# Two-block transformer on one core: the second block's first adaptation summed by VectorE in the first feed-forward

## What is computed

```python
def adaln(cond, w, b):
    m = jax.nn.silu(cond) @ w + b
    return jnp.split(m, 3, axis=-1)
...
    shift, scale, gate = adaln(c[:, None, :], w_ada, b_ada)
    cshift, cscale, cgate = adaln(c_ctx, w_ada, b_ada)
    h = rms_norm_2(x, norm_g) * (1 + scale) + shift
```

```python
    h = rms_norm(x, ln2_gain)
    x = x + jnp.square(jax.nn.relu(h @ w_up)) @ w_down
```

## Time and profile before

| | |
|---|---|
| median of three runs | 1077.58 us |
| span of the profiled execution | 1076.1 us |
| own time of the profiled execution | not listed; the runs are 1077.52, 1077.58 and 1077.97 us |
| TensorE busy | 1051.7 us, 98% |
| weight loads of TensorE | 900.5 us, 84% |
| VectorE busy | 751.0 us, 70% |
| ScalarE busy | 549.1 us, 51% |
| GpSimd busy | 63.4 us, 6% |
| mean transfer rate | 170 GB/s |
| L326, all adaptations (half of them of `ab_ada`) | 192 rows |
| ScalarE waiting for TensorE ahead of L242 | 317.5 us |

### The profile page before, as it was taken

One profiled execution on the slowest core, in us unless ns is written; L12 is line 12 of the kernel. 1 busy time (PEld: TensorE's weight loads), 2 busy tenths in 40 slices (PEclk: granted clock), 3 DMA queues, 4 the chain that ended last, 5 costly groups with the idle time before them and its releaser, 6 DMA issues. The chain is left out here.

```text
span 1076.1 us, 17324 instructions
## 1 busy us (share of the span) xinstructions
PE 1051.7 (98%) x6788; PEld 900.5 (84%) x6788; DVE 751.0 (70%) x1442; ACT 549.1 (51%) x993; POOL 63.4 (6%) x80
## 2 busy tenths in 40 slices
PE   8999999999999999999999999999999999999996
PEld 7877889899988886888998899888886687989865
DVE  5766757655556576777788888789898945824765
ACT  5543845544445454764444544452657833623563
POOL 1000000000000000001000000020051301000000
PEclk9999999999999999999999999999999999999998
DMA  9758056565564657325856566593326233943200
GB/s 344 263 197 344 3 157 195 162 201 191 192 196 163 196 196 266 120 84 185 185 196 196 160 199 197 189 305 133 110 93 260 78 118 107 257 140 118 60 21 40
DMA packets 55477, 183.33 MB, mean 170 GB/s; under 512 B 21092, under 2 KB 33764, under 8 KB 35940
## 3 DMA queue, kind: packets, MB, share of 16 engines
q1 hardware_dynamic: 55396, 182.22, 51.8%
HBM read 179.31 MB, written 2.90 MB: 169 GB/s over the span
## 5 line engine op out<-in xcount | busy, mean ns | idle before, releaser
L257 DVE TENSOR_TENSOR w_lo<-ring,w_hi 128x1024 fp32r<-128x1024 f32 x259 | 316.2, 1223 | 179.8 <-ACT w_hi L242 176.2
L242 ACT CAST w_hi<-ring 128x1024 fp32r<-128x1024 f32 x259 | 270.9, 1054 | 318.0 <-PE banks L313 317.5
L313 PE MATMUL banks<-f_hi,w_hi 128*128 128x256 f32 x512 | 144.0, 281 | 0.0
L313 PE MATMUL banks<-f_hi,w_lo 128*128 128x256 f32 x512 | 143.8, 281 | 0.0
L313 PE MATMUL banks<-f_lo,w_hi 128*128 128x256 f32 x512 | 143.8, 281 | 0.0
L313 PE MATMUL banks<-w_hi,u_hi 128*128 128x512 f32 x256 | 100.1, 391 | 0.0
L313 PE MATMUL banks<-w_hi,u_lo 128*128 128x512 f32 x256 | 99.9, 390 | 0.0
L313 PE MATMUL banks<-w_lo,u_hi 128*128 128x512 f32 x256 | 99.9, 390 | 0.0
L313 PEld LDWEIGHTS banks<-f_hi,w_hi 128*128 128x128 f32 x512 | 96.4, 188 | 0.7 <-DVE f_lo L444 0.2
L313 PEld LDWEIGHTS banks<-f_lo,w_hi 128*128 128x128 f32 x512 | 96.5, 188 | 0.5
L313 PEld LDWEIGHTS banks<-f_hi,w_lo 128*128 128x128 f32 x512 | 96.5, 188 | 0.0
(11 more groups left out here) (421 smaller groups left out, 2167.9 us busy)
## 6 DMA issues: line engine op xcount, KB each, us to landing
ring<-in_w_up SPq DMA_DIRECT2D x32, 1024.0 KB, 5.2
ring<-in_w_down SPq DMA_DIRECT2D x32, 1024.0 KB, 5.1
ring<-in_w_in SPq DMA_DIRECT2D x23, 1024.0 KB, 5.2
ring<-in_ab_ada SPq DMA_DIRECT2D x12, 1024.0 KB, 5.9
ring<-in_cd_ada SPq DMA_DIRECT2D x12, 1024.0 KB, 5.2
ring<-in_cd_in SPq DMA_DIRECT2D x12, 1024.0 KB, 5.6
ring<-in_w_out SPq DMA_DIRECT2D x8, 1024.0 KB, 7.5
ring<-in_ab_in SPq DMA_DIRECT2D x16, 512.0 KB, 4.8
```

Of the source, the lines that this page charges most:

```text
L242: nc.scalar.copy(w_hi[:, n % PARTS, :], part_source(key, q)).then_inc(hi_ready, 1)
L257: nc.vector.tensor_tensor(w_lo[:, n % PARTS, :], part_source(key, q), w_hi[:, n % PARTS, :].bitcast(F32), ALU.subtract).then_inc(part_read ...
L313: mm = nc.tensor.matmul(dst, a, b, start=first_one and i == 0, stop=last_one and i == 2, skip_group_check=shares_bank)
```

## The change

The adaptation of the second block's first layer leaves TensorE's preparation stages and goes to VectorE in the first layer's feed-forward:

* The three slabs per layer (`ada_turn`, `ada_small`, `ada_mix`) with their copies, turnings and bias sums are gone. Their twelve halves now stand in the ring's list between the halves of the first feed-forward, one behind every second or third (`ADA_BEHIND`).
* `adapt_on_vector`: for each half, four chunks of 128 x 512 weights times the condition of each partition, for the two conditions, added up over all eight chunks in `ada_sums` (128 x 6 x 2 x 512). Two such operations follow a split of VectorE where `ops_behind` says so, 96 in all. An operation waits for the one two before.
* `sum_partitions`: the sums over the 128 partitions by TensorE, with a column of -0.5 (32 times) as the stationary side and the sums as the moving side, four products in four column groups for two slabs. Two of three such sums run within the last slab of the feed-forward, the third after it in the place of the filler products.
* ScalarE copies the rows (1024 wide, then 512 wide). SyncE stores them in HBM (`row_sums`, four transfers), waits at the head of the next stage until they have landed, and fetches them back in feature order, 3072 single floats in each of two transfers (`columns_of_rows`). VectorE adds the bias in the second layer's preparation stage.
* ScalarE takes the square in both feed-forwards, and both squares of the context's rows in the first.

```diff
+ADA_SLABS = 3 * D // BANK
+ADA_BEHIND = [3 + (9 * m + 2) // 4 for m in range(2 * ADA_SLABS)]
...
+        def adapt_on_vector(dve, sums_of, done):
+            n = 0
+            for m, i in enumerate(ada_at):
+                for kk in range(KC // 2):
+                    k = m % 2 * (KC // 2) + kk
+                    w = ring[:, i % SLOTS, kk * BANK:(kk + 1) * BANK]
+                    if kk == 0:
+                        half_here(dve, i)
+                    for v in range(2):
+                        to, factor = sums_of[:, m // 2, v, :], cond[:, k, v:v + 1]
+                        if k == 0:
+                            last = nc.vector.tensor_scalar(to, w, factor, None, ALU.mult)
+                        else:
+                            dve.wait_ge(done, n - 1)
+                            last = nc.vector.scalar_tensor_tensor(out=to, in0=w, scalar=factor, in1=to, op0=ALU.mult,
+                                                                  op1=ALU.add)
+                        last.then_inc(done, 1)
+                        n += 1
+                        if kk == KC // 2 - 1 and v == 1:
+                            dve.wait_ge(done, n)
+                            dve.sem_inc(half_used, 1)
+                        yield
+
+        def ops_behind(half, part):
+            return 2 * sum((half, part) in ((b - 1, 1), (b, 0), (b, 1), (b + 1, 0)) for b in ADA_BEHIND)
+
+        def sum_partitions(pe, sums_of, r, bank):
+            for j in range(COL_GROUPS):
+                rows = slice(j * GROUP_COLS, (j + 1) * GROUP_COLS)
+                mm = nc.tensor.matmul(banks[rows, bank, :], minus_half[:, 0:1].broadcast_to([P, GROUP_COLS]),
+                                      sums_of[:, 2 * r + j // 2, j % 2, :], start=True, stop=True)
+            return mm
+
+        def columns_of_rows(sp):
+            sp.wait_ge(rows_out, 16 * COL_GROUPS)
+            for v in range(2):
+                sp.dma_start(ada[:, 0, :, v], row_sums[v].rearrange("r s n -> (r s n)").rearrange("(c p) -> p c", p=P),
+                             allow_slow_non_contiguous=True).then_inc(columns_here, 16)
...
                 def _(sp):
                     norm["sync"](sp)
+                    if layer:
+                        columns_of_rows(sp)
                     sp.dma_start(gn_gain[:], dram["gn_gain"][layer:layer + 1, :].broadcast_to([P, RET_H * HD])
...
-                    adapt_products(pe, ada_key, 0, 7)
...
-                    pe.wait_ge(kept, 1)
-                    turn_conditions(adapted(0), banks[:, 7, :]).then_inc(turned, 1)
...
-                    pe.wait_ge(ada_ready, 1)
-                    adapt_products(pe, ("ada_small", layer), 0, 7, signal=False)
...
-                    dve.wait_ge(turned, 1)
-                    add_biases(0, 3 * layer, banks[:, 7, 0:16]).then_inc(ada_ready, 1)
                     if layer:
-                        dve.wait_ge(ada_ready, 1)
+                        dve.wait_ge(columns_here, 32)
+                        step(nc.vector.scalar_tensor_tensor(
+                            out=ada[:, 0, :, :], in0=ada[:, 0, :, :], scalar=-2.0,
+                            in1=feats2[:, 0:4 * ADA_SLABS].unsqueeze(2).broadcast_to([P, 4 * ADA_SLABS, 2]), op0=ALU.mult,
+                            op1=ALU.add))
                         find_scales(0)
...
-                adapt_products(pe, ada_key, 0, ADA)
                 for h in range(RET_H):
                     values_of(h)
...
-                turn_conditions(adapted(1), banks[:, ADA_TURNED, 0:16])
                 turn_heads(2)
-                turn_conditions(adapted(2), banks[:, ADA_TURNED, 16:32]).then_inc(mix_turned, 1)
...
+                    if not beside:
+                        sp.wait_ge(rows_kept, 2)
+                        for j in range(COL_GROUPS):
+                            sp.dma_start(row_sums[j % 2:j % 2 + 1, :, j // 2, :],
+                                         summed_rows[j * GROUP_COLS:j * GROUP_COLS + 1, :, :]).then_inc(rows_out, 16)
...
+                            if not beside and i == 2 * FFN_GROUPS - 1 and q == 0:
+                                pe.wait_ge(relu_ready, FFN_GROUPS)
+                                pe.wait_ge(adapted, 64)
+                                for r in range(2):
+                                    sum_partitions(pe, ada_sums, r, r).then_inc(rows_summed, 1)
...
                     if not beside:
-                        keep_busy(0, 4)
+                        pe.wait_ge(adapted, 96)
+                        sum_partitions(pe, ada_sums, 2, 2).then_inc(rows_summed, 1)
                         return
...
+                        act.wait_ge(relu_ready, g + 1)
+                        if g >= 1:
+                            act.wait_ge(u_ready, g)
+                        nc.scalar.activation(square[:], relu[:], ACT.Square).then_inc(square_ready, 1)
                         act.wait_ge(square_ready, g + 1)
                         nc.scalar.copy(u_hi[:, g % 2, :, :], square[:]).then_inc(high_ready, 1)
...
-                            rows["square_scalar"]()
+                            rows["square_both"]()
...
+                    if not beside:
+                        act.wait_ge(rows_summed, 2)
+                        nc.scalar.copy(summed_rows[:, 0:2, :], banks[:, 0:2, :]).then_inc(rows_kept, 1)
+                        act.wait_ge(rows_summed, 3)
+                        nc.scalar.copy(summed_rows[:, 2, :], banks[:, 2, :]).then_inc(rows_kept, 1)
...
-                        nc.vector.tensor_tensor(square[:], relu[:], relu[:], ALU.mult).then_inc(square_ready, 1)
...
+                            advance(adaptation, ops_behind(2 * i + q // 2, q % 2))
```

More of the change, by code:

```diff
@@ L127, in slab_plan @@
                     halves.append((name, at + (W_IN_AT[i] if name == "w_in" else i), c0, HALF))
-    return halves, first, first_part
+                if key == ("ffn", 0) and len(half_at[key]) - 1 in ADA_BEHIND:
+                    m = len(ada_at)
+                    ada_at.append(len(halves))
+                    halves.append((ADA_NAMES[0], m // 2, m % 2 * HALF, HALF))
+    return halves, first, first_part, half_at, ada_at
 def build_program(nc, dram, out):
-    plan, first, first_part = slab_plan()
+    plan, first, first_part, half_at, ada_at = slab_plan()
     with ExitStack() as ctx:
@@ L209, in load_first_part, with load_behind @@
             sp.dma_start(ring[:, 0, cols], dram[name][at, :, cols]).then_inc(first_parts_here[q], 16)
-        def load_behind(sp, key, n_slabs, halves=2):
-            for i in range(first[key], first[key] + halves * n_slabs):
+        def load_behind(sp, key, n_slabs, between=0):
+            for i in range(first[key], first[key] + 2 * n_slabs + between):
                 load_half(sp, i + SLOTS)
@@ L223, in part_source @@
         def part_source(key, q):
-            return ring[:, (first[key] + q // 2) % SLOTS, (q % 2) * PART:(q % 2 + 1) * PART]
+            return ring[:, half_at[key][q // 2] % SLOTS, (q % 2) * PART:(q % 2 + 1) * PART]
         def split_hi(act, key, q):
@@ L237, in split_hi @@
             elif q % 2 == 0:
-                half_here(act, first[key] + q // 2)
+                half_here(act, half_at[key][q // 2])
             if n >= PARTS:
@@ L2201, in _ @@
                 def _(sp):
-                    for i in range(first["ada_turn", layer], first["ada_mix", layer]):
+                    for i in range(first["cmp_k", layer], first["w_out", layer]):
                         load_half(sp, i + SLOTS)
@@ L2420, in compress_and_retain @@
             kept_sums = sums[:, 40:40 + NR]
-            ADA, ADA_TURNED = 6, 5
-            ada_key = ("ada_mix", layer)
             def faded_of(h):
@@ L2799, in _ @@
                         ctx_gate(1)
+                    adaptation = iter(()) if beside else adapt_on_vector(dve, ada_sums, adapted)
                     for i in range(2 * FFN_GROUPS):
@@ L2804, in _ @@
                             advance(taps, 2)
+                            advance(adaptation, ops_behind(2 * i + q // 2, q % 2))
                         if i >= 1 and FFN_ORDER[i - 1][0] == "w_up":
                             activate(FFN_ORDER[i - 1][1])
-                        if not beside and i == 2:
-                            dve.wait_ge(loaded, n_loaded[0])
-                            rows["square_vector"]()
                         split_own(split_lo, dve, key, 4 * i + PARTS)
                         advance(taps, 2)
+                        advance(adaptation, ops_behind(2 * i + 1, 1))
                     advance(taps)
```

51 lines of the change are left out of this document (22 added, 29 removed).

## The result

The changed kernel takes **1080.06 us** (median of 20 runs, 1078.4 to 1083.78), the kernel before, on the same chips, 1078.09 (median of 20, 1077.52 to 1079.11): ratio 1.0023, 95% interval 1.0014 to 1.0031. The forecast was 1074.8. The change is slower by 2 us, and it has lost the steadiness of the kernel before. Its runs lie in groups that go with TensorE's mean granted clock: 1078.4 to 1078.8 at 0.994 or 0.995, 1079.2 to 1080.5 at 0.991 or 0.992, and five of the 20 at 1083.3 to 1083.8 with a clock of 0.986. Two runs fit no group, 1079.44 and 1081.56, both at 0.994. The kernel before is at 0.996 to 0.999 in all its runs with a recorded clock. The profiled execution took 1080.07 us at 0.992, with a span of 1078.3 against 1076.1.

What follows compares the result with a forecast made beforehand. TensorE, busy 98% of the span, was taken to bound the kernel. Terms -7.3 + 1.85 + 2.7 = -2.8 us on the span of 1076.1, plus 1.5 around it, gave 1074.8 us; own range 1073.3 to 1076.3, wide range 1071.0 to 1080.5.

Steps and rivals of the forecast that it cites:

- the clock: Rival: new TensorE gaps at the tail and in each layer halve its clock; +3 or so, 1078, chance 0.15.
- The argument "against": Against the clock rival: nothing followed the kernel end's gap where the clock fell; no row has a gap followed by work.
- Removal, -7.3: Adaptation slabs and turnings leave TensorE's two preparation stages: -7.3 us for both layers, bounds 0 and 16.0.
- worth nothing: Removing the last two turnings, 1.6 us before the attention: no gain, TensorE then idling about 2 us for retained rows.
- Two partition sums, +1.85: Two partition sums inside the feed-forward's last slab cost TensorE +1.85 us, bounds 0 and 9.5.
- Third, free in the gap: Third partition sum replaces four filler products at the feed-forward's end: 0.93 us against their 1.05.
- Tail, +2.7: Third sum's copy and SyncE's four store issues delay the feed-forward's stage end: +2.7 us.
- The bound of 3.2: Upper bound in us on the feed-forward tail's cost, if each handover is slow.
- VectorE, 0: 96 added VectorE operations in the feed-forward, 0.68 us each, fit beside the weight splits: cost 0.
- the rival: VectorE falls behind in the feed-forward: from 0.72 us per operation the lead is eaten; at 0.80, 1078.8; chance 0.10.
- Squares to ScalarE, 0: Feed-forward and context-row squares move from VectorE to ScalarE, which has room: cost 0.
- Fetch of the columns, hidden: SyncE's fetch of 6144 single floats in the second projection takes 7.4 us, hidden with 10 us to spare.

Runs made afterwards that it cites:

- e2: Changed kernel plus 8 idle TensorE products ahead of the attention's scores in both layers; 1078.2 us.
- e3: Changed kernel with the third partition sum made beside the other two, SyncE's stores moved to the next stage's start, column fetch behind that stage's weights; 1079.49 us.
- e4: e3 plus 8 idle products ahead of the attention's scores in both layers; 1078.18 us.
- e8: Changed kernel with 84 of VectorE's 96 multiply-adds left out, signals kept; one execution, 1081.87 us.
- e1: Changed kernel plus 14 idle TensorE products behind the third partition sum at the first feed-forward's end; 1079.42 us.
- e5: e3 with the column fetch issued between the fourth and fifth of the second projection's twelve weight loads; 1074.64 us.
- e10: Kernel before without the second block's first adaptation in the preparation stages (products, copies, turnings, biases), its weights still loaded; 1072.95 us.
- e6: e5 plus 8 idle products ahead of the attention's scores in both layers; 1073.26 us.
- e7: e6 with the third partition sum behind the feed-forward's last product and its copy by ScalarE at the next stage's start; 1072.55 us, ratio 0.9950.
- e9: Changed kernel plus 14 idle products at the tail and 8 ahead of the attention's scores in both layers; 1076.73 us, ratio 0.9991.
- e11: e10 plus 8 idle products ahead of the attention's scores in both layers; 1071.53 us.
- e12: e7 with ScalarE's two squares of the context rows one slab later in the first feed-forward; 1071.78 us, ratio 0.9943.

## Why the prediction was wrong

The step that failed is **the weight given to the clock**. It stood among the rivals as a chance of 0.15, at the price of +3 for one place, and the forecast had no term for it, though the sum itself made the waits that bring it: three of them, 3.1 us at the tail and 2 us in each layer. The wide range of 1071.0 to 1080.5 does hold the result, but a kernel that gets slower by way of the clock had a chance of 0.02 in it. In the 14 profiled executions the runs show:

- Waits of 3.25 to 4.25 us of TensorE inside the program (changed kernel, e2, e3, e4, e8): 5, and the clock fell behind every one, for 1.6 to 2.5 us each.
- Waits of 2.0 us ahead of the attention (changed kernel, e1, e3, e5, e8, e10): 12, and it fell behind 6. Cost 0.3 (e5), 1.9 (three times), 3.6 and 3.7.
- The same place filled to 0.25 us (e2, e4, e6, e7, e9, e11, e12): 14, and it fell behind none.

So the median lost 3.3 us to the waits that idle products fill (1080.06 against e9's 1076.73), more than the whole plain gain. The argument "against" in the forecast was that behind the only gap in the kernel before nothing followed, and that no row has a gap with work behind it. That is no evidence, and the second half is not even so: at the program's start TensorE waits 2.96 us, and then the first layer's 16 transposes take 3.31 us.

```profile
5.52 3.31 PE L538 MATMUL banks<-ident,x 128*128 128x128 f32 x16
```

The same 16 take 1.94 at full clock and 3.65 behind the changed kernel's tail. That reads as half clock, though the profile's clock column has 1.00 for this stretch.

The Trainium skill (TensorE: Matmul & The Clock Gate, HAM oscillation) was named in the forecast for its rule that idle gaps throttle the clock. The traces agree behind the waits over 3 us (5 of 5), and in half of the cases behind those of 2 us (6 of 12).

By the steps, as the prediction put them:

- **Removal, -7.3.** Right: -3.73 and -3.72, e10 alone -3.80. The wait of 2 us was seen, and priced as "worth nothing". By the clock it cost up to 3.7.
- **Two partition sums, +1.85.** Right: the 16 rows are 1.92 long, and the next product starts 1.85 behind their start. **Third, free in the gap.** 1.06 long instead of 0.93, and not free as placed, because its copy and stores hung behind it; e7, which takes both out of the gap, is 0.66 below e6, where it stands among the products.
- **Tail, +2.7.** Mis-sized, the second step that failed: +4.05. Counted from the start of the last ordinary product, the third sum ended after 1.38 us (341.35 - 339.97), not 1.16 (340.95 - 339.79); an issue took 2.79 / 4 = 0.70 instead of 0.50, 0.8 for the four; the handovers behind the last one took 0.78, not 0.39. The copy came 0.1 sooner. The bound of 3.2 was too low.
- **VectorE, 0.** Right in the sum (e8, for 84 of the 96), although an operation took 0.748 us, over the 0.72 at which the rival let the lead be eaten. TensorE waited for it nowhere but for ScalarE's delay.
- **Squares to ScalarE, 0.** Wrong by little on both sides. The context rows' squares cost 0.42 to 0.7 (e12). Behind the second out-projection's end the changed kernel gained 0.8; e10, which leaves the squares on VectorE, has 581.6 there, as before. It is not VectorE's sums: without them (e8) the gain is there too, 607.5 us from the second out-projection's start to the end, against the change's 607.8 and the 608.6 of the kernel before. That it is the move of the squares was not tried by itself.
- **Fetch of the columns, hidden.** Right at its place: with the clock kept (e1) the stretch over the second projection is 65.25, as before. At another place (e3, e4) it cost 3 us, not by its traffic but by the time at which SyncE is free again.

With these sizes the plain sum is -1.8 us instead of -2.8: the median before, 1078.09, less 1.8 is 1076.3, the upper end of the forecast's own range (1073.3 to 1076.3). e9 measured 1076.73, with a fall left in its profile. So even with the waits filled the gain is 1 to 2 us instead of 2.8, for the tail above all.

## What to carry to other kernels

A wait on TensorE that "costs nothing" because something else is late anyway cost up to 3.7 us here by what the clock does to the work behind it. When a change takes work out of such a place, put idle products into the wait, few enough to end before it does (longer ones were not tried), and compare the spread of runs as well as the median. Whatever makes one queue late to a meeting of all engines (here four, then two transfers issued by SyncE) belongs in the middle of a stage, between waits that the queue has anyway. And when a profile shows a mechanism that nothing in the kernel yet triggers, price it by what follows the new wait: the missing row is no argument against it, and the program's start may hold it.

## What was not expected of the hardware

- A wait of the same 2.0 us at the same place is followed by a fall in one execution, or one layer, and not in another (6 of 12), and the cost of a fall runs from 0.3 to 3.7 us. The dearest two (e1 and e8) stay at half clock for some 10 us, e5's, the cheapest, for some 3.
- The clock fell twice with next to no wait, in e9 and e12, at the start of the stage behind the second feed-forward; ahead of it TensorE works without a break on short products (adaptation, turnings of 4 columns, idle products). e12's row and stretches:

```profile
699.62 3.53 PE L579 MATMUL banks<-ident,mixed 128*128 128x128 f32 x16 [0.32 <-PEq L2662]
```

```profile
698.00:700.00 2.00, 1.69 (x14) 1.52 (x15) 1.29 (x3) 0.91 (x1) 0.03 (x1) 0.94 1.03 337
700.00:702.00 2.00, 2.00 (x11) 2.00 (x10) 1.97 (x4) 1.53 (x4) 0.20 (x2) 0.50 1.10 371
```

e7 runs the same rows at 1.94 and full clock. What decides it stays open. It may be part of what is left of the spread in e6, e9 and e11; no profile caught one of their slowest runs. It is not all of it: e9 has a run of 1078.41 at a mean clock of 0.997, beside 1075.62 at the same clock, so most of these 2.8 us have another source, which no run here shows.
- Four issues of small stores from SyncE (3 x 512 floats each) took 0.70 us each, where loads of 1 MB took 0.50.
